# A diffusion transformer block on one NeuronCore: the later row blocks of w_ada summed on VectorE, in other places, and whole weight transfers

## The reference, cut to what matters

```python
s_lat = silu(c); s_ctx = silu(c_ctx)
m_lat = split(s_lat @ w_ada + b_ada, 6)        # w_ada: 2048 x 12288; six parts of 2048
m_ctx = split(s_ctx @ w_ada + b_ada, 6)
a_lat = rms_norm(x, norm_mix) * (1 + m_lat[1]) + m_lat[0]
a_ctx = rms_norm(ctx, norm_mix) * (1 + m_ctx[1]) + m_ctx[0]
_, y = hgrn2_mixer(a_ctx, a_lat, ...)          # 16 heads, two directions, gated recurrence
h = x + m_lat[2] * y                           # y = (normed readout * silu(gate)) @ w_o
h = h + m_lat[5] * swiglu(rms_norm(h, norm_ffn) * (1 + m_lat[4]) + m_lat[3])   # hidden 5632
out = rms_norm(h, final_norm)
```

## Time and profile before

| | |
|---|---|
| median of 3 runs | 2059.31 us (2055.5 to 2062.55) |
| the profiled execution's own time | 2057.11 us |
| its span, first to last instruction | 2055.0 us |
| mean granted TensorE clock | 0.972 |
| busy: TensorE, VectorE, ScalarE, GpSimd | 1886.8, 1300.1, 1018.9, 366.1 us |
| moved by DMA | 353.26 MB, mean 172 GB/s |

### The profile page before, as it was taken

One profiled execution on the slowest core, in us unless ns is written; L12 is line 12 of the kernel. 1 busy time (PEld: TensorE's weight loads), 2 busy tenths in 40 slices (PEclk: granted clock), 3 DMA queues, 4 the chain that ended last, 5 costly groups with the idle time before them and its releaser, 6 DMA issues.

```text
span 2055.0 us, 32575 instructions
## 1 busy us (share of the span) xinstructions
PE 1886.8 (92%) x13348; PEld 1714.6 (83%) x13348; DVE 1300.1 (63%) x1867; ACT 1018.9 (50%) x1325; POOL 366.1 (18%) x140
## 2 busy tenths in 40 slices
PE   5667989898989999999988999999999999999998
PEld 3116888878787878888788997999999999999997
DVE  5586478878787878888786446544444444444445
ACT  4556465655565656555554445433433333344444
POOL 0001453443444444433400000000000000000000
PEclk9888999999999999999989999999999999999999
DMA  9997555444445444454534764677777777666773
GB/s 255 259 239 200 191 175 164 152 160 145 155 157 164 154 156 151 156 162 134 159 100 114 198 183 125 179 182 182 184 185 185 183 182 182 179 181 184 183 185 113
DMA packets 181655, 353.26 MB, mean 172 GB/s; under 512 B 19010, under 2 KB 86915, under 8 KB 180867
## 3 DMA queue, kind: packets, MB, share of 16 engines
q1 hardware_dynamic: 181506, 351.19, 61.0%
HBM read 346.92 MB, written 4.19 MB: 171 GB/s over the span
## 4 chain that ended last, share of the span: by engine, by line
PE 70%; DVE 10%; ACT 9%; DMA 6%; issue 3%; POOL 1%; SPq 1%; POOLq 0%; ACTq 0%; DVEq 0%
PE bank L1053 16%; PE bank L1055 16%; PE bank L1054 16%; DVE wlo L655 5%; DMA raw<-in_w_ada_dram 4%; ACT whi L405 3%; PE score L1155 2%; PE bank L1088 2%; PE bank L1089 1%; PE bank L1090 1%; PE score L1053 1%; PE score L1055 1%; PE score L1054 1%; DMA aw<-in_w_ada_dram 1%; PE bank L1180 1%
## 5 line engine op out<-in xcount | busy, mean ns | idle before, releaser
L655 DVE TENSOR_TENSOR wlo<-raw,whi 128x1024 fp32r<-128x1024 f32 x520 | 708.0, 1362 | 654.1 <-ACT whi L405 653.3
L1053 PE MATMUL bank<-ahi,whi 128*128 128x256 f32 (+1 forms) x2912 | 895.4, 307 | 36.9 <-DVE wlo L655 20.5
L405 ACT ACTIVATE whi<-raw 128x1024 fp32r<-128x1024 f32 x520 | 550.5, 1059 | 732.4 <-PE bank L1055 493.8
L1054 PE MATMUL bank<-alo,whi 128*128 128x256 f32 (+1 forms) x2912 | 884.0, 304 | 0.0
L1055 PE MATMUL bank<-ahi,wlo 128*128 128x256 f32 (+1 forms) x2912 | 883.9, 304 | 0.0
L1053 PEld LDWEIGHTS bank<-ahi,whi 128*128 128x128 f32 x2912 | 561.6, 193 | 74.1 <-DVE wlo L655 30.3
L1055 PEld LDWEIGHTS bank<-ahi,wlo 128*128 128x128 f32 x2912 | 561.9, 193 | 20.7
L1054 PEld LDWEIGHTS bank<-alo,whi 128*128 128x128 f32 x2912 | 562.0, 193 | 17.7
L374 POOL TENSOR_TENSOR aacc<-aw,aacc 128x1024 f32<-128x1024 f32 x128 | 358.3, 2799 | 472.9 <-ACT aw L419 472.0
L419 ACT ACTIVATE aw<-aw,cs 128x1024 f32<-128x1024 f32 x128 | 146.4, 1144 | 103.5 <-DMA aw<-in_w_ada_dram 103.4
L1088 PE MATMUL bank<-whi,ahi 128*128 128x256 f32 x512 | 155.6, 304 | 31.1 <-DVE wlo L655 18.1
(11 more groups left out here) (197 smaller groups left out, 1921.9 us busy)
## 6 DMA issues: line engine op xcount, KB each, us to landing
aw<-in_w_ada_dram SPq DMA_DIRECT2D x128, 512.0 KB, 4.8
raw<-in_hg_w_in_dram SPq DMA_DIRECT2D x192, 256.0 KB, 3.1
raw<-in_ffn_w_gate_dram SPq DMA_DIRECT2D x176, 256.0 KB, 3.9
raw<-in_ffn_w_up_dram SPq DMA_DIRECT2D x176, 256.0 KB, 4.0
raw<-in_ffn_w_down_dram SPq DMA_DIRECT2D x176, 256.0 KB, 4.0
raw<-in_w_ada_dram SPq DMA_DIRECT2D x128, 256.0 KB, 5.4
raw<-in_hg_w_f_dram SPq DMA_DIRECT2D x128, 256.0 KB, 3.1
raw<-in_hg_w_o_dram SPq DMA_DIRECT2D x64, 256.0 KB, 4.2
```

The costliest lines, as they stand in the source:

```text
L405: act.activation(whi[:, ck % SPL, :], raw[:, ck % RAW, :], ACT.Copy).then_inc(s_hi, 1)
L655: dve.tensor_tensor(wlo[:, ck % SPL, :], raw[:, ck % RAW, :], whi[:, ck % SPL, :].bitcast(F32), ALU.subtract).then_inc(s_lo, 1)
L1053: pe.matmul(dst, w, ah, start=start, stop=False, skip_group_check=True)
L1054: pe.matmul(dst, w, al, start=False, stop=False, skip_group_check=True)
```

## The change

1. The sums of the later blocks move to VectorE. For each block it runs one instruction: the first of a group writes `aacc = aw * silu(c)`, the other 15 `aacc = aw * silu(c) + aacc`. ScalarE's products, GpSimd's clearing and its additions are gone, and GpSimd has no instruction left.
2. The blocks stand in other places. `ada_chunk(i)` gives the chunk of a block. Groups 0 to 4 end their sums at chunks 34, 54, 82, 102 and 131 after C_B, the last of these in the gates; group 5 lies in the gates and ends at 150. Groups 0, 2 and 4 have a block in about every second chunk; groups 1, 3 and 5 have 16 blocks in 18, 18 and 17 chunks. Groups 6 and 7 stand in the FFN, one block every fifth chunk, from its chunk 12. In VectorE's queue a block stands behind the chunk's `lo` and recurrence steps, and ahead of `values` or `clip_gates`.
3. A block's load is issued with chunk `ada_chunk(i - 2) + 5`, after that chunk's own load.
4. `sum_modulation(e)` comes two chunks after the group's last block, for groups 6 and 7 into the bank `mx`; `add_modulation` one chunk later. The waits ahead of the next writes of those banks move with them.
5. `two` becomes `whole`: one DMA of 128 partitions for each chunk of w_ada, the gates, w_o and the FFN. `raw_landed` counts 16 for such a chunk and 32 for one of the pairs.

```diff
-            def two(slot, dst, src):
-                sp.dma_start(dst[0:64], src[0:64]).then_inc(s_raw[slot], 16)
-                sp.dma_start(dst[64:P], src[64:P]).then_inc(s_raw[slot], 16)
+            def whole(slot, dst, src):
+                sp.dma_start(dst, src).then_inc(s_raw[slot], 16)
...
-                i = ck - C_B - 6
-                if 0 <= i < PADA:
+                for i in ada_loads(ck):
...
-        @block.gpsimd
-        def _(pool):
-            pool.wait_ge(s_at, 4)
-            for e in range(8):
-                if e:
-                    pool.wait_ge(s_ap, e)
-                for k in range(KD):
-                    i = e * KD + k
-                    if k == 0:
-                        pool.memset(aacc[:, :], 0.0).then_inc(s_az, 1)
-                        pool.wait_ge(s_az, e + 1)
-                    else:
-                        pool.wait_ge(s_ac, i)
-                    pool.wait_ge(s_am, i + 1)
-                    pool.tensor_tensor(aacc[:, :], aw[:, i % 2, :], aacc[:, :], ALU.add).then_inc(s_ac, 1)
...
-            def ada_product(i):
-                act.wait_ge(s_aw[i % 2], 16 * (i // 2 + 1))
-                act.activation(aw[:, i % 2, :], aw[:, i % 2, :], ACT.Copy,
-                               scale=cs[:, i % KD, 0:1]).then_inc(s_am, 1)
...
+            def ada(i):
+                e, k = divmod(i, KD)
+                dve.wait_ge(s_aw[i % 2], 16 * (i // 2 + 1))
+                if k == 0:
+                    if e:
+                        dve.wait_ge(s_ap, e)
+                    else:
+                        dve.wait_ge(s_at, 4)
+                    dve.tensor_scalar(aacc[:, :], aw[:, i % 2, :], cs[:, k, 0:1], None, ALU.mult).then_inc(s_ac, 1)
+                else:
+                    dve.wait_ge(s_ac, i)
+                    dve.scalar_tensor_tensor(out=aacc[:, :], in0=aw[:, i % 2, :], scalar=cs[:, k, 0:1], in1=aacc[:, :],
+                                             op0=ALU.mult, op1=ALU.add).then_inc(s_ac, 1)
...
+                for e in ada_ends(ck - 1):
+                    add_modulation(e)
                 for j, n in tasks:
                     scan(j, n)
+                for i in ada_blocks(ck):
+                    ada(i)
                 if kind == "Z" and r == 0:
                     values(u)
...
             def sum_modulation(e):
                 pe.wait_ge(s_ac, KD * (e + 1))
-                pe.wait_ge(s_zc, 4 * (e + 1))
+                if e < 5:
+                    pe.wait_ge(s_zc, 4 * (ADA_ENDS[e] // 16))
+                elif e == 5:
+                    pe.wait_ge(s_gev, 4)
+                elif e == 7:
+                    pe.wait_ge(s_av, 7)
...
+def raw_landed(ck):
+    return sum(32 if C_B <= c < C_G else 16 for c in range(ck % RAW, ck + 1, RAW))
+
+ADA_ENDS = (34, 54, 82, 102, 131, 150)
+
+def ada_chunk(i):
+    e, k = divmod(i, KD)
+    if e >= 6:
+        return C_FF + 12 + 80 * (e - 6) + 5 * k
+    begin = ADA_ENDS[e - 1] + 1 if e else 4
+    return C_B + begin + k * (ADA_ENDS[e] - 2 - begin) // (KD - 1)
+
+def ada_loads(ck):
+    return [i for i in range(PADA) if (ada_chunk(i - 2) + 5 if i >= 2 else C_B + 5) == ck]
+
+def ada_ends(ck):
+    return [e for e in range(PADA // KD) if ada_chunk(KD * e + KD - 1) + 2 == ck]
```

More of the change, by code:

```diff
@@ L306, in load @@
                     col = (q + 2) % 4 * CW
-                    two(slot, dst, wada[k, :, col:col + CW])
+                    whole(slot, dst, wada[k, :, col:col + CW])
                 elif ck < C_G:
@@ L320, in load @@
                     col = 2 * D + u * 512
-                    two(slot, d3, win[:, 2 * r:2 * r + 2, col:col + 512])
+                    whole(slot, d3, win[:, 2 * r:2 * r + 2, col:col + 512])
                 elif ck < C_FF:
                     k, half = divmod(ck - C_WO, 2)
-                    two(slot, dst, wo[k, :, half * CW:(half + 1) * CW])
+                    whole(slot, dst, wo[k, :, half * CW:(half + 1) * CW])
                 elif ck < C_DN:
@@ L327, in load @@
                     d3 = dst.rearrange("p (k n) -> p k n", k=2)
-                    two(slot, d3, wgu[u % 2][:, 2 * r:2 * r + 2, (u // 2) * 512:(u // 2) * 512 + 512])
+                    whole(slot, d3, wgu[u % 2][:, 2 * r:2 * r + 2, (u // 2) * 512:(u // 2) * 512 + 512])
                 else:
                     k, half = divmod(ck - C_DN, 2)
-                    two(slot, dst, wdn[k, :, half * CW:(half + 1) * CW])
+                    whole(slot, dst, wdn[k, :, half * CW:(half + 1) * CW])
             for ck in range(CHUNKS):
@@ L898, in add_modulation @@
                 o = 2 * KD + 8 * e
-                dve.tensor_tensor(v, bank[3][:, 0:8], bias[:, o:o + 8], ALU.add).then_inc(s_av, 1)
+                dve.tensor_tensor(v, ada_sum(e)[:, 0:8], bias[:, o:o + 8], ALU.add).then_inc(s_av, 1)
             for ck, kind, u, r, tasks in positions():
@@ L1063, in chunk @@
                             scan(j, n)
-                        if sum_at(ck) is not None:
-                            sum_modulation(sum_at(ck))
+                        for e in ada_ends(ck):
+                            sum_modulation(e)
                     k = 2 * r + a
@@ L1177, in sum_modulation @@
                 pe.wait_ge(s_ac, KD * (e + 1))
-                pe.wait_ge(s_zc, 4 * (e + 1))
+                if e < 5:
[4 more added lines that the diff above has]
+                    pe.wait_ge(s_av, 7)
                 for f in range(8):
-                    last = pe.matmul(bank[3][:, f:f + 1], aacc[:, f * P:(f + 1) * P], ones[:, 0:1], start=True, stop=True)
+                    last = pe.matmul(ada_sum(e)[:, f:f + 1], aacc[:, f * P:(f + 1) * P], ones[:, 0:1], start=True, stop=True)
                 last.then_inc(s_ap, 1)
@@ L1221, in _ @@
                     pe.wait_ge(s_lo, ck + 1)
[L1222 removed]
+                    wide(ck, k, half, KF - 1, {0: (s_fgs, 2 * FG), 4: (s_fh, 2 * FG - 1), 6: (s_fh, 2 * FG), 8: (s_hr, 1), 12: (s_av, 8)})
             for k in range(KD):
@@ L1244, in _, with ada_blocks, ada_ended @@
                     last.then_inc(s_ft, 1)
[L1246 to L1256, removed]
+def raw_landed(ck):
[7 more added lines that the diff above has]
+    return C_B + begin + k * (ADA_ENDS[e] - 2 - begin) // (KD - 1)
+def ada_blocks(ck):
+    return [i for i in range(PADA) if ada_chunk(i) == ck]
+def ada_loads(ck):
+    return [i for i in range(PADA) if (ada_chunk(i - 2) + 5 if i >= 2 else C_B + 5) == ck]
+def ada_ends(ck):
+    return [e for e in range(PADA // KD) if ada_chunk(KD * e + KD - 1) + 2 == ck]
+def ada_ended(ck):
+    return sum(ada_chunk(KD * e + KD - 1) + 2 < ck for e in range(PADA // KD))
 LAST_BANK_FIRST = [14, 15] + list(range(14))
```

26 lines of the change are left out of this document (11 added, 15 removed).

## The result

The changed kernel takes 1994.9 us (median of 4 runs, 1992.16 to 1996.21) against 2059.7 before: a ratio of 0.9687, 95% interval 0.9669 to 0.9705. The forecast was 2000. The profiled execution took 1992.16 us with a span of 1990.4, against 2055.0 before.

What follows compares the result with a forecast made beforehand. TensorE, busy 92%, was taken as the bound, losing time mainly in the pair loop to late `wlo`, column sums and slow clock. Terms -25 + 5 - 18 - 21 + 12 - 9 - 3 + 1 = -58 took 2057.1 to 1999, called 2000 (1982 to 2016).

Steps and rivals of the forecast that it cites:

- what the profile was to show: Among others: pair loop clock near 1.00, TensorE idle there about 30 us, modulation stage without ScalarE waits for rows.
- the three signs of being wrong: VectorE waits for `aw` over 20 us in all; halves did not set the rate; fused instruction over 1.4 us.
- Part 5: Modulation stage: whole transfers bring rows faster than halves, until the `whi` cycle limits; -9 us (bounds -1, -19).
- Part 3: Pair loop: column sums at the new place never wait; -18.4 us of waits, -21 of slow clock (bounds -8, -25).
- Parts 1 and 2: Pair loop: VectorE regains 116 us from GpSimd, spends 96 on blocks; `wlo` waits -25 us, values and queries +5.
- a little: Pair loop: what VectorE regains on small instructions, beyond the 116 us on named forms; no size given.
- What counts is where they stand: Pair loop: VectorE does no more work over the whole loop, so the blocks' places in its queue count.
- A block at chunk 0 "costs nothing": Pair loop: a block at a pair's chunk 0 lies in VectorE's wait for the last Z product; cost zero.
- Part 4: First part of the output gates: 16 blocks of 1.2 us on VectorE with 14 us idle; +12 us (0 to +30).
- late blocks: Rival, dense groups: VectorE waits for blocks' loads, with `lo` behind; gain gone or about 2107 us; chance 0.05.
- given back: Rival, dense groups: relief at `wlo` only moves the wait to values, scores and turned keys; -30, 2029 us; chance 0.17.
- Part 6: L725's first set shortens, -3 us; in the FFN 32 blocks are hidden except beside `hidden` twice, +1 us.

Runs made afterwards that it cites:

- experiment 1: Changed kernel with each weight chunk again in two transfers, partitions 0 to 63 and 64 to 127: 2013.2 us.
- experiment 2: Changed kernel with each weight chunk in two transfers, each of all 128 partitions and half the columns: 1994.8 us.
- experiment 5: Experiment 3 with column sums reading the identity matrix, so TensorE waits for no addition; later modulation parts are not computed: 2022.6 us.
- experiment 3: Kernel before the change with whole transfers alone: 2046.2 us.
- experiment 6: Changed kernel's VectorE sums and whole transfers, with blocks and column sums at the places of before: 2043.8 us.
- experiment 4: Changed kernel with its places for blocks, loads and column sums, but ScalarE multiplying and GpSimd adding as before: 2028.2 us.
- experiment 8: Experiment 7 with other group ends, so that group 5 has two blocks in the gates in place of 16: 1986.0 us.
- experiment 10: Experiment 9 with other group ends, leaving five blocks in the gates in place of 16: 1982.2 us.
- experiment 11: Changed kernel with two GpSimd additions of 448 elements, results unread, behind each block: 2055.9 us.
- experiment 7: Changed kernel with values and the clipping of gates ahead of the same chunk's blocks in VectorE's queue: 1983.3 us.
- experiment 9: Experiment 7 with the first block nine chunks behind chunk 64 in place of four: 1975.3 us.

## Why the prediction was right

**The total and the stages.** -64.6 us against -58, and the pair loop and the gates came out within 3 us. The stage that was mis-sized most is the modulation stage: -16 us in place of -9. In the pair loop two larger errors cancel (below), so that its -58.3 for -59 is luck in part. Of what the profile was to show, a clock near 1.00 in the pair loop (it is 0.98), some 30 us of idle time of TensorE there (38) and no wait of ScalarE for rows (9.6 us) did not come. None of the three signs of being wrong came.

**Part 5, whole transfers: mechanism right, size too small.** With two normalisations the cycle was to be 2.03 us and is 1.92: the sum took `wlo` at its whole 1.23 us, and the trace above has the next instruction 1.13 us after it begins (113.29 to 114.42). Without normalisations it was to be 1.93 us at clock 0.81; it is mostly 1.6 to 1.9, around the 1.77 that the forecast had for full clock. The clock of the stage rose to 0.92. What raised it was not tested: TensorE idles 40 us of 99, no smaller share than the 44 of 113 before. ScalarE's wait for rows fell from 47.6 to 9.6 us, the stage by 13.8. Another 1.9 us come ahead of chunk 0, which the forecast had not looked at: its rows stand behind x in the queue. Experiments 1 and 2 show the cause of the faster rows: coverage of all partitions. By the Trainium skill, page "SBUF — State Buffer", section Door 1, a transfer to partitions 0 to 63 reaches only half of the ports; the traces agree so far as the rate goes, 247 GB/s with halves by partition and 283 with halves by column.

**Part 3, the column sums: mechanism right, size too large.** The waits are gone. The forecast priced them, with their slow clock, at 18 + 21 = 39 us; experiment 5, which takes away these waits alone, gains 24 in the total. Of the slow clock between chunks 72 and 195 (29.0 us lost) 15.4 came back, for 21 forecast. Of the seven stretches at the lower level that are left, five lie at waits for values, of 1.65 to 4.35 us.

**Parts 1 and 2: the cause wrong, and the size too small.** I took late `wlo` for the work of GpSimd beside VectorE, and let its end give 25 us less 5. The waits did move like that: `wlo` -22, values and queries +8. VectorE's books closed as forecast for the forms that I had named, 117 us returned for 116, and the blocks took 98 for 96. But VectorE's busy time in the loop's windows fell by 58 us (650.8 to 592.5), not by 20, so some 38 us more came back from smaller instructions, which I had called "a little".

The engine is not what shortened the loop most. In us:

| kernel, all with whole transfers | chunks 72 to 79 | chunks 80 to 191 | blocks in 80 to 191 |
|---|---|---|---|
| GpSimd, old places (experiment 3) | 45.0 | 762.3 | 112 |
| the same, sums that wait for nothing (5) | 45.7 | 741.7 | 112 |
| VectorE, old places (6) | 61.2 | 746.6 | 112 |
| GpSimd, new places (4) | 52.7 | 704.9 | 72 |
| VectorE, new places (the changed kernel) | 50.8 | 700.2 | 72 |

Behind chunk 80 the waits of the column sums are worth 20.6 us (experiments 3 and 5). Another 36.8 fall between experiments 5 and 4, which have the same engines and differ in the number and the spread of blocks, in when their rows are loaded and in where the column sums stand. What is left for the engine is 4.7 us at the new places and about 16 at the old ones. In the new places only 76 blocks lie in chunks 72 to 191 where 120 lay, three of the five groups there leave chunks free, and a column sum comes when its group has long been done. Number and spread I did not separate. An estimate from experiments 8 and 10: behind chunk 80 they have 11 and 12 blocks more than 7 and 9 and take 5.0 and 10.0 us more, 0.45 to 0.8 us a block, which for 40 blocks gives 18 to 33 of the 36.8.

The step that failed is the price: -25 us for `wlo` from what VectorE gets back of GpSimd. "What counts is where they stand" was right, but I did not price the number of blocks. Between chunks 72 and 195 experiment 3 takes 834.9 us, experiment 5 809.1 and the changed kernel 770.8: 26 us for the sums' waits where 39 were forecast, and 38 for all else where 20 were. The two errors have opposite signs.

Where then does the change of engine pay? In the gates (142.6 to 128.0) and the FFN (527.0 to 515.4) as against the same places with the old engines, and 7 us in the loop: 33 in all. The old engines put a product of 1.14 us and its wait for rows ahead of `hi`, and the chunks are shorter there (4.6 us in the gates and 2.9 in the FFN, for 6.3 in the pair loop); that this is the reason is argued, not shown. How much of this is ScalarE's and how much GpSimd's is not parted there; experiment 11 has GpSimd's instructions alone, at 15.5 and 8.1 us, on a VectorE that carries the blocks as well.

**A block at chunk 0 "costs nothing": wrong at two of four.** I read VectorE's waiting for the last Z product ahead of the clipping as cover. At chunks 96 and 144 TensorE's wait for clipped gates is 0.95 us, hardly more than the 0.9 of a pair's first chunk without a block. At chunks 112 and 160, where a dense group has blocks in the chunks just ahead too, VectorE comes late, and the wait is 2.7 us; with the block behind the clipping it is 1.5 (experiment 7).

**Part 4, the gates: right in kind,** +9.4 for +12, VectorE busy 81.3 of 86 us. Blocks did not come late: VectorE waited 3.5 us for rows in the whole run, 2.95 of it at the start, ahead of the values for chunk 72. Rival "late blocks" is out for the changed kernel, though its mechanism shows in experiment 6, with 14.9 us of such waits. So is "given back" as a whole, though its mechanism is the one that left 17.7 us of waits for values.

**Part 6, the FFN: too low.** +4.7 for +1. I wrote that the eight sums stay and two move to the FFN, and forgot to move their 1.8 us each from the one stage to the other. In the total it cancels.

## What to carry over

When a queue is in order, work that nobody waits for at once has to stand behind what others wait for: the same 128 instructions cost 20 us more ahead of two small copies and at a crowded start (experiments 7 and 9). How many such pieces fall into the tight stage, and where, mattered more here than which engine runs them; move some to a stage where that engine idles, but not so far that another stage becomes the dense one (experiments 8 and 10). And where rows set the pace, as in the modulation stage, a load split by partition halves is slower than one split by columns.

## What was not expected of the hardware

- Two GpSimd additions of 448 elements behind each of 128 VectorE instructions cost 61 us in all, 0.48 us a block, though GpSimd's results are not used; some VectorE instructions with operands in SBUF grow by 0.6 to 0.7 us beside them (0.69 to 1.31, 0.48 to 1.15), others do not (L755, 0.68).
- The scan with a shifted first operand took 3360 ns beside GpSimd and 1198 without.
- Transfers of 64 partitions hold a stage at 247 to 250 GB/s with the engines' share at 1.00 to 1.02; the same bytes as two transfers of 128 partitions pass at 283 with a share of 0.88.
